# A decoder kernel on one core: the parameter tile is made 288 columns long, so that the tiles behind it begin 64 bytes further on

## The chip, the cores and the metric

The kernel runs on one core of a Trainium2 chip. The metric is the time of one execution in microseconds of device time, the median over several runs. The profile, the trace and every duration below come from one profiled execution of the kernel before.

## The reference

The reference is two transformer-like blocks one after the other, on 256 tokens of width 1024, in float32. Each block has a token mixer and then a layer of small experts, cut here to what matters:

```python
# block 1: modulation vectors from c, pooling mixer and a state-space mixer, then peer
mod = (silu(c) @ w_ada + b_ada).reshape(B, 6, D)
h = modulate(rmsnorm(x, norm_mix), shift_m, scale_m); proj = h @ w_in
x = x + gate_m * (concat([pool_mixer(...), ssd_mixer(...)]) @ w_out)
x = x + gate_f * peer(modulate(rmsnorm(x, norm_ffn), shift_f, scale_f), ...)
# block 2: a gated linear recurrence and a gated convolution, then peer
h = h + token_mixers(rmsnorm(h, norm1), w_in_2, ..., w_out_2)
h = h + peer_2(rmsnorm(h, norm2), ...); return rmsnorm(h, final_g)

def peer(h, w_query, keys, expert_down, expert_up):
    q = h @ w_query                      # 8 heads, two halves of 128
    scores against 128 + 128 keys, top 16 of each, top 16 of the 256 sums, softmax -> gates
    u = expert_down[idx]; act = gelu(h . u);  v = expert_up[idx]; out = sum(gates * act * v)
```

There are 16384 experts of 1024 numbers each in both tables of both blocks.

## The kernel before

**Dense instead of gathered.** The kernel does not gather experts. It multiplies the activations with the whole table `down` (64 pairs of 128x1024 blocks per layer), takes the gelu, multiplies with a gate that is zero where an expert was not chosen, and multiplies with the whole table `up` (64 pairs again). Two peer layers make 256 blocks of `down` and 256 of `up`, each of 512 KB.

**Three products for one.** To get float32 accuracy from TensorE's fast format, every operand is split into a high part (rounded to float32r) and a low part (what the rounding left out). `product` (lines 550 to 555) then issues three matmuls of float32r operands into the same accumulator: low times high (L553), high times low (L554), high times high (L555). Each pass loads a 128x128 stationary operand (LDWEIGHTS, PEld in the profile) and streams the moving one through (MATMUL, PE).

**The ring.** Weights come through three tiles of three slots of 4096 bytes per partition: `ring` (what a DMA of the SP queue brings), `ring_hi` (ScalarE rounds it, `make_high`, L365) and `ring_lo` (VectorE subtracts, `make_low`, L371). `split_linear` walks over the eight 128-column chunks of a block; it waits on `low`, and its last matmul signals `block_used`, on which the next ScalarE copy into that slot waits. The SP queue waits for `make_low` before it overwrites a slot.

**What is stationary and what moves.** There are three kinds of `product` matmuls:

- stationary a chunk of `ring_hi` or `ring_lo`, moving 256 columns of `h_hi` or `h_lo`: the projections of block 1 (`w_in`), its queries (`wq0`), both `down` tables, 48 of the 56 blocks of `w_in2`, and `w_out2`. 352 blocks of 24 matmuls.
- the same, but moving 256 columns of `w_hi`, `w_lo` or `xs_lo` (`xs_hi` in the code uses `w_hi` and `w_lo` as room for the scaled input): the first 8 blocks of `w_in2` and the 16 blocks of `wq1`. 24 blocks of 24 matmuls.
- stationary 128 columns of `w_hi` or `w_lo`, moving 512 columns of `ring_hi` or `ring_lo`: both `up` tables (`up`, from L879).

In both peer layers the pairs of `down` blocks 0 to 37 run while VectorE finds the top scores; from pair 38 on float16 matmuls that build the gates (L847) stand between the blocks.

**Where the tiles lie.** All tiles are taken in order of declaration by `sb` (lines 91 to 119), one behind the other in each partition; a tile's start is rounded up to 32 bytes. `xT` starts at byte 1152. From the declared lengths follow the starts, and the rest that each leaves when divided by 256 (below called its phase):

| tile | first byte before | phase before |
|---|---|---|
| `xT`, `h_hi`, `h_lo` | 1152, 9344, 17536 | 128 |
| `prm` (270 columns, 1080 bytes) | 25728 | 128 |
| `cst` | 26816 | 192 |
| `ring`, `ring_hi`, `ring_lo` | 28864, 41152, 53440 | 192 |
| `arena` (all other activations) | 65728 | 192 |
| `wf`, `w_hi`, `w_lo` | 196800, 200896, 204992 | 192 |
| `sel16`, `mod`, `xs_lo` | 209088, 213952, 214464 | 192 |

Slots of the ring are 4096 bytes apart, its chunks 512 bytes, and the chunks of `h_hi`, `h_lo`, `xs_lo` 1024 bytes; none of these steps changes a phase.

Of the kernel before, what the change touches and what calls it, by code (L numbers as in the profile page):

```python
# [5 lines left out]
P = 128  # L6
# [37 lines left out]
NCOL = _at  # L44
# [5 lines left out]
def decoder_kernel(nc, A, out):  # L50
# [11 lines left out]
    with ctx:  # L62
        def sb(name, shape, dt=fp32):
            return ctx.enter_context(nc.sbuf_tensor(name, shape, dt))
# [27 lines left out]

        h_hi = sb("h_hi", [P, KC, T], fp32r)
        h_lo = sb("h_lo", [P, KC, T], fp32r)
        prm = sb("prm", [P, NCOL])
        cst = sb("cst", [P, NCONST])
        ring = sb("ring", [P, RING, BLK])
        ring_hi = sb("ring_hi", [P, RING, BLK], fp32r)
# [1953 lines left out]
```

## Time and profile before

| | us |
|---|---|
| median of 3 runs | 2038.16 |
| lowest and highest run | 2026.67, 2045.39 |
| the profiled execution, its own time | 2028.78 |
| its span from first to last instruction | 2027.0 |
| PE busy in it | 1974.7 (97%) |
| PEld, DVE, ACT busy | 1830.3, 1506.5, 1013.7 |

PE is the matrix multiplication of TensorE, PEld its loading of stationary operands, DVE is VectorE, ACT is ScalarE. Matmuls are pipelined: a record of one lasts longer than the distance to the next, so the pace of TensorE is read from starts, or from counts over a stretch, and not from the duration of one record. "Who waited for whom" and the chain of work that ended last are inferred from semaphores. A few matmul records can be missing.

### The profile page before, as it was taken

To read this page: it belongs to the slowest core of one execution; us is meant where nothing else is said; L and a number is where in the kernel's file an instruction comes from. 1 tells how busy PE (TensorE), PEld (TensorE's weight loads), DVE (VectorE), ACT (ScalarE), POOL (GpSimd) and SP (SyncE) were. 2 spreads that over 40 slices of the span, in tenths; PEclk is the share of its full clock that TensorE was granted. 3 is DMA by queue.
4 is the path that set the end of the run, shared out by engine and by line. 5 is a ranking of instruction groups with operands and counts; after the bars stand their busy time and mean duration, and the time that the engine had idled before them with its cause. 6 is when DMAs were issued, how large, how long until landed. Compare 5 with 4: busy or idle time off the path is not lost.

```text
span 2027.0 us, 37752 instructions
## 1 busy us (share of the span) xinstructions
PE 1974.7 (97%) x14131; PEld 1830.3 (90%) x14131; DVE 1506.5 (74%) x2593; ACT 1013.7 (50%) x1358; POOL 0.2 (0%) x4
## 2 busy tenths in 40 slices
PE   7999899999999999999999999999999999999998
PEld 6988899999999888888799999999999998888886
DVE  5766769987886666666679665699878866666666
ACT  3651444455555444454546554444555554444444
POOL 0000000000000000000000000000000000000000
PEclk8999999999999999999999999999999999999999
DMA  7645767776556778777655654788766567777776
GB/s 269 207 169 206 270 194 249 243 240 213 182 182 212 244 238 243 240 241 244 209 167 155 189 158 145 229 248 240 242 209 183 181 214 242 240 242 240 237 246 197
DMA packets 135020, 440.82 MB, mean 217 GB/s; under 512 B 14976, under 2 KB 15232, under 8 KB 131200
## 3 DMA queue, kind: packets, MB, share of 16 engines
q1 hardware_dynamic: 117056, 406.84, 64.4%
q10 hardware_dynamic: 17856, 32.51, 4.4%
q8 instruction: 71, 1.16, 0.3%
q14 instruction: 37, 0.30, 0.0%
HBM read 403.64 MB, written 35.65 MB: 217 GB/s over the span
## 4 chain that ended last, share of the span: by engine, by line
PE 89%; DVE 6%; DMA 3%; ACT 2%; issue 1%; SPq 0%; DVEq 0%; ACTq 0%
PE ps L553 27%; PE ps L554 27%; PE ps L555 27%; PE ps L847 3%; DVE ring_lo L371 2%; DMA ring<-in_w_in 2%; PE ps L590 1%; ACT ring_hi L365 1%; PE ps L696 1%; DVE arena L1840 1%; PE ps L823 1%; PE ps L546 0%; DMA ring<-in_down 0%; DVE arena L1351 0%; DMA xT<-kept_x_spill 0%
## 5 line engine op out<-in xcount | busy, mean ns | idle before, releaser
L371 DVE TENSOR_TENSOR ring_lo<-ring,ring_hi 128x1024 fp32r<-128x1024 f32 x632 | 772.4, 1223 | 298.4 <-ACT ring_hi L365 290.4
L365 ACT ACTIVATE ring_hi<-ring 128x1024 fp32r<-128x1024 f32 x632 | 668.1, 1057 | 623.5 <-PE ps L555 470.3
L553 PE MATMUL ps<-h_hi,ring_lo 128*128 128x256 f32 x2816 | 799.0, 284 | 20.4 <-DVE ring_lo L371 9.4
L554 PE MATMUL ps<-h_lo,ring_hi 128*128 128x256 f32 x2816 | 786.8, 279 | 0.0
L555 PE MATMUL ps<-h_hi,ring_hi 128*128 128x256 f32 x2816 | 786.7, 279 | 0.0
L553 PEld LDWEIGHTS ps<-h_hi,ring_lo 128*128 128x128 f32 x2816 | 535.5, 190 | 24.9 <-issue 20.8
L554 PEld LDWEIGHTS ps<-h_lo,ring_hi 128*128 128x128 f32 x2816 | 535.2, 190 | 0.4 <-issue 0.2
L555 PEld LDWEIGHTS ps<-h_hi,ring_hi 128*128 128x128 f32 x2816 | 532.7, 189 | 0.0
L555 PE MATMUL ps<-ring_hi,w_hi 128*128 128x512 f32 x1024 | 398.4, 389 | 0.0
L554 PE MATMUL ps<-ring_lo,w_hi 128*128 128x512 f32 x1024 | 398.4, 389 | 0.0
L553 PE MATMUL ps<-ring_hi,w_lo 128*128 128x512 f32 x1024 | 398.4, 389 | 0.0
L553 PEld LDWEIGHTS ps<-ring_hi,w_lo 128*128 128x128 f32 x1024 | 192.2, 188 | 40.2
L554 PEld LDWEIGHTS ps<-ring_lo,w_hi 128*128 128x128 f32 x1024 | 192.2, 188 | 39.8
L555 PEld LDWEIGHTS ps<-ring_hi,w_hi 128*128 128x128 f32 x1024 | 192.2, 188 | 39.7
L1192 ACT ACTIVATE w_hi<-wf 128x512 fp32r<-128x512 f32 x128 | 80.9, 632 | 240.6 <-DVE wf L1751 240.6
L1765 DVE TENSOR_TENSOR w_lo<-wf,w_hi 128x512 fp32r<-128x512 f32 x128 | 88.6, 693 | 91.0 <-ACT w_hi L1192 91.0
L1722 DVE TENSOR_TENSOR xT<-iota,sel 128x1024 f16<-128x1024 f16 x128 | 87.8, 688 | 27.7 <-PE ps L847 27.6
L1730 DVE TENSOR_TENSOR xT<-xT,sel 128x512 f16<-128x512 f16 x256 | 93.2, 419 | 1.5
L1751 DVE TENSOR_TENSOR wf<-xT,arena 128x512 f32<-128x512 f32 x124 | 84.7, 683 | 0.0
L1166 ACT ACTIVATE arena<-ps 128x512 f32 (+1 forms) x128 | 71.2, 591 | 26.9 <-ACT wf L1154 24.8
L1154 ACT ACTIVATE wf<-ps 128x512 f32<-128x512 f32 x128 | 74.3, 580 | 0.0
L847 PE MATMUL ps<-xT 128*128 128x128 f16 x1024 | 72.1, 220 | 0.0
(284 smaller groups left out, 1287.7 us busy)
## 6 DMA issues: line engine op xcount, KB each, us to landing
ring<-in_down SPq DMA_DIRECT2D x256, 512.0 KB, 4.3
ring<-in_up SPq DMA_DIRECT2D x256, 512.0 KB, 4.0
ring<-in_w_in SPq DMA_DIRECT2D x80, 512.0 KB, 3.7
kept_z<-wf ACTq DMA_DIRECT2D x124, 256.0 KB, 3.3
xT<-kept_z SPq DMA_DIRECT2D x124, 256.0 KB, 4.3
arena<-in_w_ada SPq DMA_DIRECT2D x24, 1024.0 KB, 10.1
ring<-in_wq SPq DMA_DIRECT2D x32, 512.0 KB, 4.3
ring<-in_w_out_ssd SPq DMA_DIRECT2D x8, 512.0 KB, 4.2
```

The costliest lines, as they stand in the source:

```text
L365: nc.scalar.activation(ring_hi[:, part_slot(m), :], ring[:, slot(m), :], ACT.Copy).then_inc(S("high"), 1)
L371: ns.tensor_tensor(ring_lo[:, part_slot(n), :], ring[:, slot(n), :], ring_hi[:, part_slot(n), :].bitcast(fp32), ALU.subtract)\
L553: mm(psum, s_lo, m_hi, start=start, stop=False)
L554: mm(psum, s_hi, m_lo, start=False, stop=False)
L555: return mm(psum, s_hi, m_hi, start=False, stop=stop)
L847: last = mm(PS[half][:, k * P:(k + 1) * P], onehot[half][:, 0, k, :, :].rearrange("p a b -> p (a b)"), weighed[half][:, part, k, :, :].rea ...
L1154: A_(wf[:, p % 2, :], PS[4 + p % 2][:, :], gelu).then_inc(S(f"act_done{l}"), 1)
L1192: A_(w_hi[:, p % 2, :], wf[:, p % 2, :], ACT.Copy).then_inc(S(f"w_high{l}"), 1)
L1722: TTn(onehot[g % 2].rearrange("p s t a b -> p (s t) a b"), iota16[:, None, :, :].to_broadcast([P, 8, HD, 2]), sel16[:, g, 0, :, :, :].rear ...
L1730: last = TTn(weighed[g % 2][:, part, :, :, :], onehot[g % 2][:, 1, :, :, :], sel16[:, g, 1, part, :, :][:, :, None, :].to_broadcast([P, 4, ...
L1751: TTn(wf[:, j % 2, :].rearrange("p (i t) -> p i t", i=2), src.rearrange("p (i t) -> p i t", i=2), g2, ALU.mult).then_inc(S(f"wf_ready{l}"), 1)
L1765: TTn(w_lo[:, p % 2, :], wf[:, p % 2, :], w_hi[:, p % 2, :].bitcast(fp32), ALU.subtract)\
```

## The change

`prm` holds 270 columns of parameters. After the change a tile of 288 columns is declared in its place and `prm` is a view of its first 270 columns. Nothing reads or writes the 18 columns behind them. Every instruction stays as it was, in number, order, shape and waits; only addresses change. `prm` itself starts where it did. It now ends at byte 26880, which is 105 times 256, so `cst` and every tile behind it start 64 bytes further on than before: those that had phase 192 now have phase 0. `xT`, `h_hi` and `h_lo` stand before `prm`; they keep their addresses and their phase 128.

```diff
@@ -92,7 +92,8 @@
         h_hi = sb("h_hi", [P, KC, T], fp32r)
         h_lo = sb("h_lo", [P, KC, T], fp32r)
-        prm = sb("prm", [P, NCOL])
+        prm_room = sb("prm_room", [P, 288])
+        prm = prm_room[:, 0:NCOL]
         cst = sb("cst", [P, NCONST])
         ring = sb("ring", [P, RING, BLK])
         ring_hi = sb("ring_hi", [P, RING, BLK], fp32r)
```

## Rows read from the trace of the kernel before

**Rows 1.** The page, part 4: the chain of work that ended last.
```profile
PE 89%; DVE 6%; DMA 3%; ACT 2%; issue 1%; SPq 0%; DVEq 0%; ACTq 0%
```

**Rows 2.** The page, part 5, groups by line: busy us, mean ns; idle before.
```profile
L371 DVE TENSOR_TENSOR ring_lo<-ring,ring_hi 128x1024 fp32r<-128x1024 f32 x632 | 772.4, 1223 | 298.4 <-ACT ring_hi L365 290.4
L365 ACT ACTIVATE ring_hi<-ring 128x1024 fp32r<-128x1024 f32 x632 | 668.1, 1057 | 623.5 <-PE ps L555 470.3
...
L554 PE MATMUL ps<-h_lo,ring_hi 128*128 128x256 f32 x2816 | 786.8, 279 | 0.0
...
L554 PE MATMUL ps<-ring_lo,w_hi 128*128 128x512 f32 x1024 | 398.4, 389 | 0.0
```

**Rows 3.** Groups by line, shapes kept apart: the product of the scaled input.
```profile
L554 PE MATMUL ps<-xs_lo,ring_hi 128*128 128x256 f32 x192 | 55.6, 290 | 0.0
```

**Rows 4.** Stretches, PE alone: length us, busy (matmuls), granted clock, DMA share, GB/s.
```profile
228.00:257.00 29.00, 29.00 (x258) 1.00 0.76 245
300.00:460.00 160.00, 160.00 (x1414) 1.00 0.78 242
...
631.00:654.00 23.00, 23.00 (x198) 1.00 0.80 259
665.00:1000.00 335.00, 335.00 (x1480) 1.00 0.77 238
1120.00:1187.00 67.00, 67.00 (x572) 1.00 0.66 195
1255.00:1271.00 16.00, 16.00 (x136) 1.00 0.42 141
```

**Rows 5.** Timeline of PE in layer 0's down pairs from 38 on: start, us.
```profile
487.03 0.28 PE L553 MATMUL ps<-h_hi,ring_lo 128*128 128x256 f32 x1
...
489.27 0.28 PE L554 MATMUL ps<-h_lo,ring_hi 128*128 128x256 f32 x1
```

**Rows 6.** The chain in order of time, two pieces of PE: start, us, what.
```profile
184.95 3.45 PE ps L590 x16
...
1018.48 3.47 PE ps L776 x32
```

**Rows 7.** Instructions on `h_lo`: ns min/median/max, first and last start, form.
```profile
L1336 DVE TENSOR_TENSOR h_lo<-arena,h_hi x4: 1216/1221/1226, 1040.2 to 1253.9; 128x1024 fp32r<-128x1024 f32 x4
```

**Rows 8.** The chain in order of time, its pieces of DMA over 3 us.
```profile
5.95 21.23 DMA ring<-in_w_in
...
103.30 8.88 DMA ring<-in_w_in
...
269.98 3.62 DMA ring<-in_down
...
1033.07 4.83 DMA ring<-in_w_in
...
1225.19 3.73 DMA ring<-in_wq
...
1282.96 3.63 DMA ring<-in_down
...
2011.18 6.25 DMA xT<-kept_x_spill
```

**Rows 9.** Two stretches of the start, ACT alone; then share and GB/s of DMA.
```profile
5.50:7.50 2.00, 0.00 (x0) 1.00 0.98 393
10.00:25.00 15.00, 1.80 (x3) 1.00 1.01 424
```

## The prediction, made before the changed kernel was run

> **What bounds the kernel now.** I read the chain of work that ended last first: 89% of it is PE, 6% DVE, 3% DMA [rows 1]. So TensorE sets the time, and I ask at what pace its matmuls follow each other and whether that pace hangs on addresses, the one thing that this change moves. Busy times don't tell the pace, since records overlap (2816 records of 279 ns, [rows 2]); I read counts over stretches in which PE never pauses [rows 4]. A record is about 0.28 us long, so about two of each count reach in from the edges and I take them off.
>
> - `wq0` and the `down` pairs before 38: 160 us / 1412 = 113.3 ns per matmul, and 29 / 256 = 113.3.
> - `down` pairs from 60 on: 23 / 196 = 117.3. Nineteen steps between 487.03 and 489.27 give 2.24 / 19 = 117.9 [rows 5]. Late `w_in2` and `w_out2`: 67 / 570 = 117.5. I take 117.8 for all.
> - `wq1`: 16 / 134 = 119.4, I take 120.
> - `up`, 512 columns: 335 / 1478 = 226.7.
>
> The clock is the full 2.4 GHz in all of them (granted 1.00). These paces are the argument. `wq0` and `wq1` are the same code: same shape, same stationary tiles, same PSUM banks. They differ in where the moving operand lies: `h_hi`, `h_lo` (phase 128) against `w_hi`, `w_lo`, `xs_lo` (phase 192, as the ring), and one runs at 113.3, the other at 120. And with the very same tiles the first kind runs at 113.3 in one stretch and 117.8 in another. So placement may have a price on TensorE, of up to 6.7 ns in 113, and there is a second influence, which is no address, since addresses don't change between pair 30 and pair 60.
>
> **What the floor looks like.** Sixteen matmuls of plain float32 with 256 columns take 3.45 us, 216 ns each [rows 6]. A float32 matmul of 256 columns needs the time of 512 float32r columns or a little less (226.7 is the `up` pace), so I take 216 as the floor of an `up` matmul. Thirty-two matmuls that load 128x128 float32 weights and stream two columns take 3.47 us, 108.4 each [rows 6]: loading alone costs that, and I take 109 as the floor of a 256-column one.
>
> **The change part by part.**
>
> *The longer tile.* No instruction, wait or DMA is added or removed, 72 bytes per partition are left unused, and no tile is crowded out. Cost 0, and nothing covers it that could go. No queue is passed by a moved step, since none is moved.
>
> *Engines other than PE.* `make_low` reads `ring` and `ring_hi`, all at phase 192: 1223 ns [rows 2]. The same operation reads `arena` (192) and `h_hi` (128) and writes `h_lo` (128) in 1221 ns [rows 7]. Mixed phases or equal ones: 2 ns in 1200. `make_high`, 1057 ns for 1024 elements, waited for PE 470 us of its 623 us of idle time [rows 2]; a few ns there are covered. If the cover were gone: 632 x 2 ns is 1.3 us. I take 0, ends -1 and +1.
>
> *DMA.* The ring is filled by descriptors of 4096 bytes, each now starting at phase 0. Where does a faster transfer show? Only in the chain's DMA pieces that end in the ring: 21.23 + 8.88 + 3.62 + 4.83 + 3.73 + 3.63 = 45.9 us [rows 8]; the seventh, 6.25 us, ends in `xT`, which does not move. At the start the DMA engines are full: 424 GB/s at a share of 1.01 with destinations at phase 192, and 393 at 0.98 while the load of `xT` (phase 128) is among them [rows 9], so per busy engine 420 against 401. The phase 192 destinations are not the slower ones. I take 0; ends 0 and -3 us.
> The Trainium skill (DMA: Bandwidth & Descriptors, How a descriptor splits into AXI transactions) has a rule for this: a transaction must start at a multiple of 256 bytes, so a descriptor that starts elsewhere pays for the bytes before it. For 4096 bytes from phase 192 that would be 134 beats instead of 128, and by that rule the 45.9 us would shrink by 4.5%, 2.1 us. The two rates above don't show it.
>
> *TensorE.* 352 x 24 = 8448 matmuls move `h` (2816 on each of three lines), 24 x 24 = 576 move the scaled input (192 on L554, [rows 3]), 3 x 1024 = 3072 are `up` [rows 2]. Of the 8448, the stages before pair 38 (24 blocks of `w_in`, 16 of `wq0`, 76 `down` blocks per layer) and a part of `w_in2` run at 113.3, about 4900; the rest, about 3500, at 117.8. The sum of what lies above the floors: `up` 3072 x 10.7 = 33 us, scaled input 576 x 11 = 6 us, `h` 4900 x 4.3 + 3500 x 8.8 = 52 us. That is 91 us, and by no row is it known how much of it is placement. Lower end: all gone, -91. Upper end: every `h` matmul goes at the 120 of `wq1`: 4900 x 6.7 + 3500 x 2.2 = 41 us.
> What I take: 0. After the change the scaled input still has the phase of the ring, and `w` that of the ring, as now; `h` keeps its own address. All starts were multiples of 64 bytes and still are. The same tiles at the same addresses show two paces, so the larger part of the spread is not set by an address alone.
> The Trainium skill speaks against any gain and any loss here: SBUF — State Buffer, Who interferes with whom, says that TensorE has two read ports of its own and never waits for anyone, and its specifications name lines of 16 bytes, which 64-byte starts respect. By that page the term is 0 exactly. The 113.3 against 120 of the same code says that the page is not the whole account.
>
> **Sum.** 0 (tile) + 0 (engines) - 1 (DMA, between 0 and -3) + 0 (TensorE) = -1 us. The profiled execution took 2028.8, the median is 2038.2, and the three runs reach from 2026.7 to 2045.4. That spread of 19 us is of the size that a swap between the two paces makes: 4.5 ns x 4900 = 22 us if all `h` matmuls slow down. I set the -1 against the median: 2037 us. A difference under 1% (20 us) can hardly be told from none with such a spread, so 1% is also my bound for "faster" and "slower".
>
> **Rivals.**
>
> *A. The phase of the moving operand counts (faster).* A stream that starts off a multiple of 256 pays, and more at 192 than at 128. For it: both kinds with moving phase 192 lie 11 ns above their floor, whether 256 columns or 512 long (120 - 109, 226.7 - 216), so a fixed sum per matmul; those with moving phase 128 lie only 4.3 or 8.8 above. After the change both kinds have phase 0: -33 - 6 = -39 us, 1999 us. Against it: the double pace at phase 128, and that 16-byte lines know nothing of 256. Should the loads of weights at phase 0 also speed up the `h` matmuls, as much as 52 us more would come, 1947.
>
> *B. The distance between the two streams counts (slower).* Weights and moving columns are read at the same time; where the tiles have equal phase (`wq1`, `up`) they collide all along and pay 11 ns, where they are 64 bytes apart (`ring` 192, `h` 128) they pay less. After the change the ring is at 0 and `h` at 128: 128 bytes apart. If places repeat every 128 bytes, that is a collision again and all `h` matmuls go at 120: +41 us, 2079. If the fast pace alone is lost (all at 117.8), 4900 x 4.5 = +22 us, 2060. It decides from about 4500 matmuls that lose 4.5 ns; then it passes 1%. If, on the other hand, 128 bytes are the better distance and the slow pace goes, 3500 x 4.5 = -16 us, 2022, which is inside 1%. Against B as a loss: nothing in the rows says which way 128 goes, and the two paces at one distance say that it isn't all.
>
> *C. The change doesn't do what it says.* The starts follow from the declared lengths (25728 + 1152 = 26880 = 105 x 256), so only a rounding of the room could undo it; under 1 in 50, and the time would be as before.
>
> **Chances.** Nothing measurable in any stage (my forecast, C in it): 48%. A: 20%, -39 us or more. B: 32%, of which a clear loss (2060 to 2079) 20%, a gain within 1% (2022) 9%, a gain over 1% (`h` at the floor) 3%. Faster by over 1%: 20 + 3, less 1 for a weaker A: 22%. Slower by over 1%: 20%. Within 1%: 58%. The range takes A's 1999 in, less 2 for DMA, and B's 2060, and leaves out its far end and A's: 1997 to 2062. The forecast's own range is 2027 to 2046, the spread of the runs.
>
> **What would show it.** Right: `wq0` at 113.3, `wq1` at 120, `up` at 226.7 in the same counts over stretches, `make_low` at 1223 ns, DMA rate of the start at 424. A is right if `up` falls towards 216 and `wq1` towards 109 while `h` stays. B is right if `up` and `wq1` stay and the pace of `h` changes in the pairs before 38. If both stay and only the share of the stages at 117.8 changes, it is the second influence. The DMA step is wrong if the first piece of 21.23 us shrinks by more than 1 us. The whole prediction is wrong if the time leaves 2018 to 2058, because then placement on TensorE was worth more than I let it.

## The result and the profile after

The changed kernel takes 2056.98 us (median of 4 runs, 2055.20 to 2058.05), the kernel before 2034.76 us (4 runs, 2026.67 to 2045.39; the 2038.16 given earlier is the median of three of them). The ratio is 1.0108, with a 95% interval of 1.0072 to 1.0144: 1% slower. The forecast was 2037 with a range of 1997 to 2062, so the time lies in the range, which reached that far because of rival B, but not at the forecast, and the change does more than nothing. The profiled execution took 2057.30 us, its span is 2055.5 us against 2027.0 before, 28.5 us more.

The chain of waits of the changed kernel (page, part 4) has the same shape as [rows 1]; the share of PE has grown by one point:

```profile
PE 90%; DVE 4%; DMA 3%; ACT 2%; issue 1%; SPq 0%; DVEq 0%; ACTq 0%
```

The other engines do what they did. These are the rows of the changed kernel that answer to [rows 2] and [rows 7] (lines are one further on: L371 is now L372):

```profile
L372 DVE TENSOR_TENSOR ring_lo<-ring,ring_hi 128x1024 fp32r<-128x1024 f32 x632 | 773.1, 1224 | 319.0 <-ACT ring_hi L366 315.8
L366 ACT ACTIVATE ring_hi<-ring 128x1024 fp32r<-128x1024 f32 x632 | 667.9, 1057 | 652.6 <-PE ps L556 548.7
...
L555 PE MATMUL ps<-h_lo,ring_hi 128*128 128x256 f32 x2816 | 796.8, 283 | 0.0
...
L555 PE MATMUL ps<-ring_lo,w_hi 128*128 128x512 f32 x1024 | 398.3, 389 | 0.0
```

```profile
L1337 DVE TENSOR_TENSOR h_lo<-arena,h_hi x4: 1217/1221/1226, 1053.7 to 1271.1; 128x1024 fp32r<-128x1024 f32 x4
```

`make_low` takes 1224 ns (1223 before), `make_high` 1057 (1057), `h_lo` from `arena` 1221 (1221), and a record of an `up` matmul 389 (389). Only the record of an `h` matmul is longer, 283 ns instead of 279. ScalarE's wait for PE grew from 470 to 549 us: it sees a slower TensorE.

Where PE never pauses, its counts tell the pace, as in [rows 4]. Stretches of the changed kernel, PE alone (length in us, busy time and matmuls, granted clock, share of the DMA engines, GB/s):

```profile
229.00:259.00 30.00, 30.00 (x253) 1.00 0.71 228
300.00:460.00 160.00, 160.00 (x1351) 1.00 0.73 228
...
670.00:1000.00 330.00, 330.00 (x1459) 1.00 0.79 241
1140.00:1190.00 50.00, 50.00 (x423) 1.00 0.65 191
1262.00:1285.00 23.00, 23.00 (x195) 1.00 0.53 157
```

With two taken off for the edges: `wq0` 30 / 251 = 119.5 ns (113.3 before), the `down` pairs 160 / 1349 = 118.6 (113.3), late `w_in2` 50 / 421 = 118.8 (117.5), `wq1` 23 / 193 = 119.2 (119.4), `up` 330 / 1457 = 226.5 (226.7). The fast pace of `h` is gone and nothing else has moved. The clock is 1.00 in each stretch.

For the whole kernel I take the distance from each start of a `product` matmul to the next one's start where that is of the same kind, and leave out the longer gaps (124 ns and more, for `up` 245), whose sum is in the last column:

```
kernel     h: mean ns, share at 115 or less   up: mean ns   xs: mean ns   longer gaps of h, us
before        115.11        60%                 226.69        119.85        61.8
changed       118.73        18%                 226.68        119.85        65.1
```

8448 x (118.73 - 115.11) = 30.6 us is what the mean step gives. All steps from one `h` matmul to the next together, the longer gaps too, take 1024.6 us against 995.6, so 29.0 us more, and the span grew by 28.5: the lost time lies there. The 18% are single steps in the uneven rhythm of the changed kernel (122, 115, 119 and the like), no stretch at 113.3.

DMA: the chain's pieces into the ring, and the filling of the ring at the start, in the changed kernel (chain in order of time; then stretches of ACT, whose last two numbers are share and GB/s of the DMA engines):

```profile
6.15 20.43 DMA ring<-in_w_in
...
104.28 8.06 DMA ring<-in_w_in
...
272.59 3.75 DMA ring<-in_down
...
1010.96 6.20 DMA ring<-in_w_in
...
1241.25 3.65 DMA ring<-in_wq
...
1300.30 3.73 DMA ring<-in_down
```

```profile
5.50:7.50 2.00, 0.06 (x1) 1.00 0.98 401
10.00:25.00 15.00, 1.21 (x2) 1.00 1.02 427
```

The six pieces sum to 45.8 us, as against 45.9 in [rows 8]. Single pieces differ by more, the first two by 0.8 us less and the fourth by 1.4 more, so the sum is a rough measure. The rate is the better one: 427 GB/s at a share of 1.02, where it was 424 at 1.01 in [rows 9]. Starts at multiples of 256 bytes gained 1% at most there.

### The profile page after: what moved, and what is told of

Read it like the earlier page. It is cut to its first block, busy times and chain, and to the rows that moved or that the text cites. A ratio compares the mean times of both kernels' runs of the same rounds, so it can differ in the third digit from the quotient of the medians.

```text
span 2055.5 us, 37752 instructions
## 1 busy us (share of the span) xinstructions
PE 2004.2 (98%) x14131; PEld 1860.8 (91%) x14131; DVE 1509.3 (73%) x2593; ACT 1013.5 (49%) x1358; POOL 0.2 (0%) x4
## 4 chain that ended last, share of the span: by engine, by line
PE 90%; DVE 4%; DMA 3%; ACT 2%; issue 1%; SPq 0%; DVEq 0%; ACTq 0%
PE ps L554 28%; PE ps L556 27%; PE ps L555 27%; PE ps L848 3%; DMA ring<-in_w_in 2%; DVE ring_lo L372 1%; PE ps L591 1%; ACT ring_hi L366 1%; PE ps L697 1%; PE ps L824 1%; PE ps L547 0%; DMA ring<-in_down 0%; DMA xT<-kept_x_spill 0%; DVE arena L1352 0%; PE ps L948 0%
## 5 line engine op out<-in xcount | busy, mean ns | idle before, releaser
L372 DVE TENSOR_TENSOR ring_lo<-ring,ring_hi 128x1024 fp32r<-128x1024 f32 x632 | 773.1, 1224 | 319.0 <-ACT ring_hi L366 315.8
L366 ACT ACTIVATE ring_hi<-ring 128x1024 fp32r<-128x1024 f32 x632 | 667.9, 1057 | 652.6 <-PE ps L556 548.7
L554 PE MATMUL ps<-h_hi,ring_lo 128*128 128x256 f32 x2816 | 808.8, 287 | 19.2 <-DVE ring_lo L372 7.7
L556 PE MATMUL ps<-h_hi,ring_hi 128*128 128x256 f32 x2816 | 797.2, 283 | 0.0
L555 PE MATMUL ps<-h_lo,ring_hi 128*128 128x256 f32 x2816 | 796.8, 283 | 0.0
```

Source lines behind the costliest of these rows:

```text
L366: nc.scalar.activation(ring_hi[:, part_slot(m), :], ring[:, slot(m), :], ACT.Copy).then_inc(S("high"), 1)
L372: ns.tensor_tensor(ring_lo[:, part_slot(n), :], ring[:, slot(n), :], ring_hi[:, part_slot(n), :].bitcast(fp32), ALU.subtract)\
L554: mm(psum, s_lo, m_hi, start=start, stop=False)
L555: mm(psum, s_hi, m_lo, start=False, stop=False)
L556: return mm(psum, s_hi, m_hi, start=False, stop=stop)
```

## The experiments

From here on the **distance** is the start of the stationary tile less that of the moving one, modulo 256: for `h` 64 before and 128 after the change, for `up` and for the scaled input 0 in both. Theory D: the distance sets the pace (rival B of the prediction). Against it stand the phase of each stream by itself (rival A), and that neither counts and the kernel merely falls on a slow rhythm.

### The two streams alone

A kernel that keeps nothing but the three matmuls of `product`, on tiles filled once, with starts that can be chosen:

```diff
+    # (columns of one matmul, first byte of the stationary streams, of the moving ones), bytes past a multiple of 4096
+    out = []
+    for d in range(0, 512, 32):
+        out.append((256, d, 0))
...
+                mm(ps, s_lo, m_hi, start=start, stop=False)
+                mm(ps, s_hi, m_lo, start=False, stop=False)
+                return mm(ps, s_hi, m_hi, start=False, stop=stop)
```

> Only TensorE's streams, nothing of the reference is computed: 96 products' matmuls per setting (72 with 512 columns), with the first byte of the stationary tiles and of the moving tiles set to chosen distances, 0 to 480 bytes. Distance theory (what counts is how far the stationary operand's start lies from the moving one's): 256-column pace 113 to 118 ns at 64 bytes, about 119 at 128, 120 at 0 and at 256; moving both streams together by 64, 128 or 192 bytes changes nothing; 512 columns 226.7 ns at 0 and less at some other distance. Phase theory (rival A turned round: a stream's own start modulo 256 counts): pace changes when both are moved together, and 512 columns go with the moving start alone. If neither: all settings within 1 ns.

Measured, 256 columns, moving start at 0 (mean time from one matmul's start to the next, ns, without the first six steps): 120.00 at distance 0, 118.30 at 32, 117.78 at 64, 118.69 at 96, 118.70 at 128, 120.03 at 160, 117.78 at 192, 116.65 at 224, and the same again from 256 to 480 (120.00, 118.30, 117.78, ... 116.65). 512 columns (here the stationary start is 0 and the moving one varies): 226.66 at distance 0 and 256, 228.9 at 192, 232.3 at 128, 233 to 234 elsewhere. Five stretches, PE alone: distance 0, 64, 128, 192, and then 64 once more with both streams moved on by 128:

```profile
35.00:46.00 11.00, 11.00 (x94) 1.00 0.01 1
58.80:69.40 10.60, 10.60 (x92) 1.00 0.00 0
82.40:93.00 10.60, 10.60 (x92) 1.00 0.01 2
106.00:117.00 11.00, 11.00 (x95) 1.00 0.00 0
271.80:282.00 10.20, 10.20 (x92) 1.00 0.00 0
```

10.60 us and 10.20 us for the same 92 matmuls: both at distance 64. The DMA engines are at rest, no other engine works, and nothing but the start addresses of TensorE's operands was set differently from one stretch to the next, so the pace hangs on these addresses, and not on traffic of others. That the two reads of TensorE get in each other's way is the likely reason, but is inferred. A period of 256 bytes is shown in these steps of 32, and that distance 64 has two paces, 117.8 and 113.3, the two of the kernel before. The phase by itself is not shown to count: with distance 0 every phase gives 120.0. At distance 64 the moving starts 0 and 64 gave 117.8, and 128 and 192 gave 113.3; whether the phase picks among the two is settled further down, where moving start 0 shows both.

### In the kernel: keep the change's phases, restore the distance

64 unused bytes ahead of the first tile instead of behind `prm`. Everything moves on by 64, the ring to phase 0 as in the changed kernel, `h` to 192; the distance stays 64.

```diff
+        low_room = sb("low_room", [P, 16])
         xT = sb("xT", [P, KC, T])
...
-        prm_room = sb("prm_room", [P, 288])
-        prm = prm_room[:, 0:NCOL]
+        prm = sb("prm", [P, NCOL])
```

> The kernel before with 64 unused bytes ahead of the first tile: every tile moves by 64 bytes, so the ring and all behind it start where they start after the change, but h and xT move too and the distance of ring and h is as before (64 bytes). Distance theory: the pace of before comes back (113.3 ns in wq0, 113.3 in the down pairs before 38), the time is within 0.5% of before, 2035 us. Phase theory: the phase 0 of the ring costs what it cost in the change, so about 2057 us, or another value if the 192 of h matters.

Measured: 2029.88 us (10 runs) against 2030.70 for the kernel before (13 runs), ratio 1.0008 (0.9984 to 1.0033).

```profile
300.00:460.00 160.00, 160.00 (x1414) 1.00 0.79 243
670.00:1000.00 330.00, 330.00 (x1457) 1.00 0.77 239
1130.00:1180.00 50.00, 50.00 (x444) 1.00 0.67 195
```

The ring is at a multiple of 256 and costs nothing; the 1% goes with the distance. And the third stretch, late `w_in2`, went at 50 / 442 = 113.1 here, where it went at 117.8 in the profile of before: with the same distance either pace can come up there. The times of the single runs spread as before's do, 2024.3 to 2045.2.

### In the kernel: other distances

`h_hi` and `h_lo` moved, and the room behind `prm` set so that the tiles from `cst` on keep phase 192. For distance 0, 64 unused bytes stand ahead of `h_hi`; for distance 192 and two more below the tiles are views into longer ones, behind 128 unused bytes ahead of `xT` (`H_AT` is 0 here):

```diff
-        h_hi = sb("h_hi", [P, KC, T], fp32r)
...
+        h_rooms = [sb(name, [P, KC * T + 64], fp32r) for name in ("h_hi", "h_lo")]
+        h_hi, h_lo = [r[:, H_AT:H_AT + KC * T].rearrange("p (c t) -> p c t", t=T) for r in h_rooms]
```

Distance 0 (`h` at phase 192):

> h_hi and h_lo moved by 64 bytes to phase 192, the ring at phase 192 as before (its start 256 bytes further): distance 0 between ring and h. Distance theory: all h matmuls at the 120 ns of wq1, so 4900 x 6.7 + 3500 x 2.2 = 41 us more than before, about 2076 us, and more than after the change. Phase theory (the ring's phase 0 is what costs): as before, 2035 us.

Distance 192 (`h` at phase 0):

> h_hi and h_lo begin at phase 0, the ring at 192: distance 192. Theory 1 (distance alone, 117.78 ns in the bare streams at 192): all h matmuls at 117.8, 4900 x 4.5 = 22 us more than 2028.8, so about 2050, a little less than the changed kernel (118.7 at distance 128, 2057). Theory 2 (the distance counts by its size to either side, so 192 is like 64): two paces, 113.3 and 117.8, about 2030.

Measured: distance 0 takes 2062.45 us (4 runs; before 2030.70), ratio 1.0155 (1.0131 to 1.0178). Distance 192 takes 2047.35 us (7 runs, 2036.36 to 2050.11; before 2028.68), ratio 1.0075 (1.0047 to 1.0103). The pairs of `down` at distance 0, and below at distance 192:

```profile
300.00:460.00 160.00, 160.00 (x1336) 1.00 0.73 228
```

```profile
300.00:460.00 160.00, 160.00 (x1361) 1.00 0.75 235
```

160 / 1334 = 119.9 ns and 160 / 1359 = 117.7, the 120.0 and 117.8 of the bare streams. For distance 0 the expectation from the profiled pace was 41 us and 32 came: the mean of all `h` steps rose by 4.69 ns (119.80 against 115.11), 39.6 us, but the longer gaps shrank from 61.8 to 55.3 us. Presumably a slower stream hides some of the waits between stages. At distance 192 the profiled run has nearly lost the fast pace, but not wholly: of the 348 blocks of `h` matmuls that run nearly without gaps 11 go at 113.3, four of the early `w_in2` among them:

```profile
1099.23 0.28 PE L556 MATMUL ps<-h_hi,ring_lo 128*128 128x256 f32 x1
...
1100.93 0.28 PE L556 MATMUL ps<-h_hi,ring_lo 128*128 128x256 f32 x1
```

These are 15 steps in 1.70 us, 113.3 ns each. So distance 192 has two paces too, as theory 2 said, though the slow one holds most of the run, as theory 1 said. One of its runs took 2036.4 and one 2040.4; that more blocks ran fast in those is likely, but they are in no trace here. In the changed kernel, at distance 128, no block goes at 113.3.

### Distances that are no multiples of 64

A finer scan of the bare streams, in steps of 4 bytes, and with high and low tiles at different distances:

> Only TensorE's streams again, nothing of the reference is computed. Stationary start less moving start in steps of 4 bytes from 0 to 252 (96 matmuls each), then the high and the low parts at different distances, 512 columns at a few small distances, and the scan in steps of 8 bytes once more from another start. Distance theory, after the first scan: the pace is a function of the distance modulo 256, 120.0 at 0, 117.8 or 113.3 at 64, 118.7 at 128, 115.6 at 8; the fine scan shows narrow good places beside the 8, and the second scan gives the same numbers, except that places with two paces (as 64) may show the other one. If the pace were set by 16-byte lines alone, all distances that are no multiple of 16 would cost the same, and those that are would be equal. 512 columns: 226.7 at 0, dearer at all other distances.

Measured: no smooth curve. 113.3 at distances 52, 76, 88 and 168, 115.6 at 8, 120 at 0, 20, 36, 84, 100 to 112, 128, 144, 156, 160, 204, 216, 228, 236, 244 and 252, 120.6 at 220, the rest between. Distance 128, 118.7 in the first scan, is 120.0 in this one: a first sign that it too has two paces. With the moving start at 128 the curve comes back in 24 of 32 distances (8: 115.55, 16: 118.36, 168: 113.34) and differs at 8 (88: 120.00 instead of 113.3). I took 168, fast in both scans, and 8, equal in both, into the kernel (`h` at phase 24 and 184):

> h_hi and h_lo begin at phase 24 and the ring at phase 192, so the stationary start lies 168 bytes behind the moving one modulo 256; up and the scaled input keep distance 0. Theory 1 (the distance alone sets the pace, and the bare streams give its size; there 168 gave 113.3 ns in both scans): all 8448 h matmuls at 113.3, also in the stages that run at 117.8 in the kernel before, 3500 x 4.5 = 16 us less than its profiled 2028.8, so about 2013 to 2020 and a small spread from run to run; wq1 and up stay at 120 and 226.7. Theory 2 (the two paces come from something else than the distance, and 113.3 is lost for a part of the run at any distance): h at 113.3 in the early stages and 117 or so late, 2027 to 2045 as before. Theory 3 (starts that are no multiples of 64 cost the product or VectorE and ScalarE something): h above 118, 2055 or more.

> h_hi and h_lo begin at phase 184, the ring at 192: distance 8. Theory 1 (distance alone, sizes of the bare streams, 115.56 ns at 8 in both scans): all 8448 h matmuls at 115.6, in every stage alike: 4900 x 2.3 more and 3500 x 2.2 less than in the profiled run before, about 4 us more than 2028.8, so 2033, with a small spread. Theory 2 (streams that start near each other collide all along, so 8 is like 0): 120 everywhere, 2062 as with distance 0.

Measured: 168 takes 2066.00 us (5 runs, ratio 1.0189, 1.0162 to 1.0216), 8 takes 2064.94 us (4 runs, ratio 1.0175, 1.0141 to 1.0209). In both the `h` matmuls of the `down` pairs go at 119.9 ns, here distance 168 and then 8:

```profile
300.00:460.00 160.00, 160.00 (x1336) 1.00 0.73 225
```

```profile
300.00:460.00 160.00, 160.00 (x1336) 1.00 0.74 228
```

Both expectations of theory D in its simple form failed, by about 50 us and by 32; the times are those of theory 3 for distance 168 and of theory 2 for distance 8. Either the start in time picks the pace at 168 too, or it matters which of the two streams leaves the multiple of 64. Two experiments tell these apart.

### How a stream starts

Six distances, each 16 times over, and ahead of each a float32 matmul whose length grows by 3 columns a round:

```diff
+    for k in range(16):
+        for d in (0, 8, 64, 128, 168, 192):
+            out.append((256, 16 + 3 * k, d, d, 0, 0))
```

> Only products are run, on tiles filled once, and none of the reference is computed. Distances 0, 8, 64, 128, 168 and 192 (stationary start less moving start, bytes), each 16 times over with 96 matmuls of 256 columns, and ahead of each a float32 matmul whose length grows by 3 columns a round, so that each stretch begins at another offset in time. Theory 1 (each distance has one pace, save 64, which can lock into either of two): 120.0, 115.6, 113.3 or 117.8 mixed, 118.7, 113.3, 117.8, the same in each of the 16. Theory 2 (the start in time picks the pace at any distance): each distance shows two or more paces, and 168 falls to 117.8 in some of its 16 too.

Measured, mean distance of starts in ns and how many of the 16:

```
distance    paces
  0         120.0 in 16
  8         115.5 in 16
 64         117.8 in 13, 113.3 in 3
128         118.7 in 9, 120.0 in 7
168         120.0 in 12, 113.3 to 113.5 in 4
192         117.8 in 16
```

Distance 64 and distance 168, each at its first pace and at its fast one (PE alone, in the order 64 slow, 64 fast, 168 slow, 168 fast; counts over stretches this short are good to 1% only):

```profile
59.00:70.00 11.00, 11.00 (x95) 1.00 0.00 0
491.90:502.40 10.50, 10.50 (x94) 1.00 0.01 2
83.10:94.00 10.90, 10.90 (x93) 1.00 0.01 2
732.50:743.00 10.50, 10.50 (x94) 1.00 0.01 2
```

The first theory's account of 64 holds, and moving start 0 shows both paces, so it is not the phase that picks. 128 has two paces as well, both slow; 113.3 came up neither in these 16 nor in any block of the changed kernel. 168 has two, and the scans had twice met the rarer one: the second theory was right about 168, though its slow pace is 120.0 and not 117.8, and my reading of two equal values as a fixed pace was wrong. Distances 0, 8 and 192 showed one pace each. For 192 sixteen restarts were not enough to find the second, which the kernel at distance 192 had shown.

That leaves distance 8, which showed one pace, 115.5, and yet went at 120 in the kernel, where the moving start was 184. So the stationary tiles are moved instead: `ring_hi`, `ring_lo`, `w_hi`, `w_lo` at phase 136, `h` at 128 (`ring` and all else behind it are at 128 too). Of the edit, this is the part for `ring_hi` and `ring_lo`:

```diff
+        ring_rooms = [sb(name, [P, RING * BLK + 64], fp32r) for name in ("ring_hi", "ring_lo")]
+        ring_hi, ring_lo = [r[:, 2:2 + RING * BLK].rearrange("p (s n) -> p s n", n=BLK) for r in ring_rooms]
```

> The distance is 8 again, but now h stays at phase 128 and ring_hi and ring_lo begin at phase 136 (w_hi and w_lo at 136 too, so that up keeps distance 0). In the kernel whose h began at 184 against a ring at 192 all h matmuls went at 120, and in the bare streams, where the moving start was a multiple of 64, 8 gave 115.55 in all 16 restarts. Theory 1 (the moving start must be a multiple of 64, then 8 has the one pace 115.55): h at 115.55 in every stage, 4900 x 2.2 more and 3500 x 2.2 less than in the profiled run before, about 2032, with a small spread. Theory 2 (in the kernel any start off a multiple of 64 costs the h matmuls the fast pace): 120, about 2062. If up slows down as well, it does so by 3072 matmuls times what it gains over 226.7, and that is told apart in its own stretch.

Measured: 2051.68 us (4 runs, 2050.68 to 2052.47; before 2033.67), ratio 1.0094 (1.0073 to 1.0115).

```profile
300.00:460.00 160.00, 160.00 (x1387) 1.00 0.77 238
700.00:1000.00 300.00, 300.00 (x1289) 1.00 0.76 234
```

160 / 1385 = 115.5 in the `down` pairs, as theory 1 had it, but `up`, whose moving tile now starts at 136, goes at 300 / 1287 = 233.1 instead of 226.7: 3072 x 6.4 = 20 us, which is the whole distance from the expected 2032. So the distance is not all. At distance 8 `h` goes at 115.5 from moving start 128 and at 119.9 from 184, and in the kernel at distance 168 (moving start 24) it never found the fast pace of the streams. For `up` both streams start at 136, so which of the two costs it is not told apart. The three odd starts, 24, 136 and 184, are multiples of 8 but not of 16 or 32, so whether a multiple of 16 or 32 would do is open.

### High and low tiles at different distances

The bare streams again, every combination of starts 0, 64, 128, 192 for three of the four tiles, four restarts each:

> Only products are run, on tiles filled once, and none of the reference is computed. The high and low stationary tiles and the low moving tile begin at 0, 64, 128 or 192 each, the high moving one at 0: 64 combinations, each with four restarts of 48 matmuls of 256 columns and one of 8 matmuls of 512. Theory 1 (each matmul pays by the distance to what is loaded beside it, whether hi or lo): the best combinations lock at 113.3 in all four restarts, and the one of the kernel before (stationary 64 beyond moving) only in some. Theory 2 (a rhythm over three matmuls picked by the start): no combination shows 113.3 in all four. For 512 columns distance 0 of both stays the best, 226.7.

Measured, the best and a few others (stationary high, stationary low, moving high, moving low; ns in the four restarts, one for 512 columns):

```
256 columns   64 192  0   0    113.34 113.34 113.46 113.44
256 columns   64  64  0   0    113.32 117.80 113.32 117.80
256 columns    0 192  0 192    115.54 115.90 115.63 115.63
256 columns  128 128  0   0    118.63 118.56 118.59 118.59
256 columns    0   0  0   0    120.00 120.00 120.00 120.00
512 columns    0   0  0   0    226.67
512 columns   64 128  0 128    228.86
512 columns    0   0  0 128    233.33
```

One of the 64 holds 113.3 to 113.5 in all four restarts: the high stationary tile at distance 64, the low one at 192. No other does. For 512 columns none beats distance 0 of all.

### A version that keeps the fast pace

`ring_lo` gets slots of 1088 columns; all blocks but those of `up` are written and read 32 columns (128 bytes) into theirs. `ring_hi` and `h` stay. `up` keeps distance 0.

```diff
-        ring_lo = sb("ring_lo", [P, RING, BLK], fp32r)
+        ring_lo = sb("ring_lo", [P, RING, BLK + 64], fp32r)
...
+        def low_part(n, a, b):
+            at = 0 if any(up_block_no(l, 0) <= n < up_block_no(l, PAIRS) for l in range(2)) else 32
+            return ring_lo[:, part_slot(n), at + a:at + b]
...
-                return ring_hi[:, part_slot(n), a:b], ring_lo[:, part_slot(n), a:b]
+                return ring_hi[:, part_slot(n), a:b], low_part(n, a, b)
```

> ring_hi stays at phase 192 and h at 128 (distance 64), ring_lo is written and read 128 bytes later in its slot for every block but those of up (distance 192 from h); up keeps distance 0 for both. In the bare streams this mixture held 113.3 to 113.5 in all four restarts, where plain distance 64 fell to 117.8 in some. Theory 1 (the mixture takes the slower of the two rhythms away): h at 113.4 in every stage, 3500 x 4.4 = 15 us less than the profiled run before, so about 2013 with a small spread. Theory 2 (an interruption can put it on the slow pace all the same, four restarts were luck): the late stages at 117.8, about 2029 and the spread of before. Theory 3 (the kernel's interruptions lead to a third, worse pace): over 2035.

And the same with `at = 32` for all blocks, `up` too:

> As the one before, but the blocks of up are also written and read 128 bytes later, so that the two moving tiles of up lie 128 bytes apart: up has distance 0 for its high part and 128 for its low part. By the bare streams with 512 columns the like of it (0, 0, 0, 128) gave 233.3 against 226.7. Theory 1: up at 233.3, 3072 x 6.6 = 20 us more than the kernel with only h mixed, so about 2033 if that one gives 2013. Theory 2 (up does not care about its low part): no difference between the two.

Measured: 2016.29 us (6 runs, 2014.89 to 2019.68) against 2032.72 for the kernel before (17 runs, 2024.09 to 2040.55), ratio 0.9924 (0.9897 to 0.9952). With `up` moved as well 2036.64 us (10 runs), ratio 1.0016 (0.9996 to 1.0036). First the kernel with `up` left alone: `down` pairs, pairs from 60 on, late `w_in2`; then the one with `up` moved, `down` pairs and `up`:

```profile
300.00:460.00 160.00, 160.00 (x1415) 1.00 0.79 243
632.00:651.00 19.00, 19.00 (x170) 1.00 0.80 251
...
1120.00:1175.00 55.00, 55.00 (x488) 1.00 0.68 199
```

```profile
300.00:460.00 160.00, 160.00 (x1414) 1.00 0.79 242
700.00:1000.00 300.00, 300.00 (x1288) 1.00 0.75 232
```

The stages that ran at 117.8 before go at 19 / 168 = 113.1 and 55 / 486 = 113.2. This version is 0.8% faster than the kernel before. Between the float16 matmuls of the gates, where [rows 5] showed 117.9, the starts are now about 113 apart:

```profile
490.02 0.28 PE L559 MATMUL ps<-h_hi,ring_hi 128*128 128x256 f32 x1
...
491.49 0.28 PE L557 MATMUL ps<-h_hi,ring_lo 128*128 128x256 f32 x1
```

13 steps in 1.47 us are 113.1. Theory 1 said 2013 and 2016.3 came; the steps of `h` take 982.5 us in all, 13.1 less than in the profiled run before, where 15 were expected. `up` moved as well costs 300 / 1286 = 233.3 against 226.7, 3072 x 6.6 = 20.3 us, and the two medians differ by 20.35.

All kernels by the starts in their traces, as in the table above. The medians come from several sessions, in which the kernel before had medians from 2028.7 to 2034.8, so compare them by the ratios given above. At distances 168 and 8 many steps are longer than 124 ns and fall among the gaps (118.2 and 84.2 us of them), so these two means are too low:

```
kernel                          h mean ns   at 115 or less   up mean ns   median us
before (distance 64)              115.11         60%           226.69      2034.76
all moved by 64 (64)              115.00         63%           226.68      2029.88
changed (128)                     118.73         18%           226.68      2056.98
distance 192                      117.65          3%           226.69      2047.35
distance 0                        119.80          0%           226.68      2062.45
distance 168, h at 24             119.80          0%           226.68      2066.00
distance 8, h at 184              119.94          0%           226.68      2064.94
distance 8, stationary at 136     115.78         63%           232.96      2051.68
high 64, low 192                  113.49         97%           226.68      2016.29
the same, and up with low 128     113.50         97%           233.33      2036.64
```

## Why the prediction was wrong

The path was read rightly: TensorE sets the time, its pace is what counts, and everything else came out as costed. The tile, VectorE and ScalarE cost nothing, `make_low` differs by 1 ns. For DMA the sum took -1 out of 0 to -3; the pieces of the chain sum to 45.8 against 45.9, so 0. By the rule of the Trainium skill (DMA: Bandwidth & Descriptors, How a descriptor splits into AXI transactions) the prediction estimated a gain of 2.1 us, and that doesn't show in this chain. The page speaks of bytes that are fetched; that the same holds for the destination in SBUF was the prediction's own reading. A packet of 4096 bytes took 159 ns (the median in the trace) with the ring at phase 192 and at phase 0.

**The step that failed** is the TensorE term: "What I take: 0." It rested on two sentences. "All starts were multiples of 64 bytes and still are" supposes that 64 is the grain; the bare streams repeat every 256 bytes and differ between the multiples of 64 (120.0 at 0, 117.8 or 113.3 at 64, 118.7 or 120.0 at 128). "The same tiles at the same addresses show two paces, so the larger part of the spread is not set by an address alone" is true only of which pace comes up at a moment, and no argument for 0: the restarts show that which paces there are to fall into depends on the distance, 117.8 and 113.3 at 64, 118.7 and 120.0 at 128. The change took away a distance at which the fast pace exists and put in its place one where it was never seen. In place of 0 stand 29.0 us by the steps of `h` in the trace, 28.5 in span and 22.2 between the medians.

The page that says that TensorE never waits for anyone (the Trainium skill: SBUF — State Buffer, Who interferes with whom) gave the term as exactly 0. Where it and the rows differ, the rows decide: with all other engines at rest the same matmuls go at 113.3 to 120.0 ns, by their addresses and by how the stream begins. The page may still be right that no other engine makes TensorE wait. That TensorE's two reads hinder each other is inferred from the dependence on the distance; no run shows a port.

**Rival B**, the distance, was right in kind, and its sign came: `up` and `wq1` stayed, and `h` before pair 38 went from 113.3 to 118.6 ns. Its smaller form ("if the fast pace alone is lost", all at 117.8) gave 2060 against 2057 measured, and that the two are so close is partly luck. It priced 22 us, where the traces show 29.0, since the matmuls that had been slow became slower too (118.7 on the mean, not 117.8); the 22.2 between the medians is smaller because the profiled run before, 2028.8, was faster than the median of its kernel. Its larger form ("if places repeat every 128 bytes", 2079) is excluded for the kernel by the mean of 118.73 against 119.80 at distance 0, though in the bare streams 128 went at 120.0 in 7 of 16 restarts. It was given 20% for a clear loss. It should have had more: of the comparisons that [rows 4] offered, `wq0` against `wq1` was the only one with the same code at different addresses, and the change altered the distance of no `product` matmuls but the 8448 of `h`, the only ones that ran at 113.3. The prediction counted the missing direction against B ("nothing in the rows says which way 128 goes"). But the rows did say where 64 stands: its fast pace was the fastest that any of them showed for this shape, 4 ns above the floor of 109, so a move away from it could gain little and lose much.

**Rival A**, the phase of the moving stream: both signs that the prediction asked for are missing, `up` stays at 226.68 and the scaled input at 119.85. The kernel with everything moved by 64 settles it: ring at phase 0, `h` at 192, and the time of before. A small part of A remains: at one and the same distance `h` went at 119.9 from moving start 184 and at 115.5 from 128, and `up` went at 233.1 with both streams at 136.

**Rival C** (no change at all) is excluded by the ratio.

The spread of the kernel before, 2026.7 to 2045.4, has a likely explanation. A start at distance 64 may take either rhythm, and with the mixture that was always fast in the streams the runs span 4.8 us (6 runs) instead of 16.5 (17 runs). At distance 192, where the kernel shows both paces too, 7 runs span 13.8 us. That the slow runs had more matmuls at 117.8 was not traced.

Open is why these distances and no others: the fine scan has no pattern that I can put into a rule, and whether every value of it holds at another restart is not known, since those of 128 and 168 did not. What in the moment of a start picks the pace is open too.

## What to carry to other kernels

Where TensorE bounds a float32r kernel with LDWEIGHTS before every matmul, the first bytes of the stationary and the moving tile are tuning parameters: note them modulo 256 for each kind of product, and treat a "harmless" alignment of one tile as a change of all its pairs. Two paces of one instruction at one address are no evidence that the address doesn't count; run the bare pair of streams with several restarts before you trust one value, and then look for it in the kernel, whose waits and other matmuls restart the stream in more ways than a test does. Start a tile that TensorE streams at a multiple of 64 bytes, since the three moving starts tried that were not (24, 136, 184) all came out slow, and look for a placement whose pace is the same in every restart, not for the one with the lowest reading.

## What the runs showed of the hardware

- Three float32r matmuls of 256 columns, each with its own stationary tile, take from 113.3 to 122 ns each by the starts of their tiles, with a period of 256 bytes in the scan in steps of 32. With 512 columns it is 226.7 at distance 0 and up to 237 at others.
- The best place depends on the shape: distance 0 is the worst of the multiples of 64 for 256 columns (120.0) and the best for 512 (226.7).
- At distances 64, 128 and 168 the pace also depends on how the stream begins (two values each), and it then holds through the stretch. At 0, 8 and 192 sixteen restarts gave one value (120.0, 115.5, 117.8), but at 192 the kernel shows 113.3 in 11 of 348 blocks.
- With the high stationary tile at distance 64 and the low one at 192 the streams gave 113.3 to 113.5 in all four restarts, and the kernel a mean of 113.5 for `h`.
- The distance does not decide alone: `h` at moving start 184 went at 119.9, where distance 8 gave 115.5 from moving start 128, and `up` with both streams at 136 went at 233.1, where distance 0 gave 226.7 with both at 192 or at 0.
- Starts at multiples of 256 bytes brought the DMAs into the ring 1% at most: 427 GB/s at a share of 1.02 against 424 at 1.01.
